# Block 2 of a two-block transformer layer: VectorE takes the next head's maximum ahead of the last head's scaling

## What is computed

```
# branch A, gated_deltanet, per chunk of 64 tokens and head
lmat = where(strict, (k*beta) @ k.T * decay, 0)
tmat = triangular_solve(lmat + eye, eye)     # inverse of a unit triangular matrix
u, w = tmat @ (v*beta), tmat @ (k*beta*exp(gc))

# branch B, dsa_sparse_attention, per block of 128 queries
score  = sum_h iw[h] * relu(iq[h] @ ik.T)    # causal
sel    = top_k(score, 128)                   # keys that are kept
logits = q_b[h] @ ckv[sel].T * R_KV**-0.5 + rel_bias[bucket(dist)]
p      = softmax(logits)                     # over the kept keys, causal
o[h]   = (p @ ckv[sel]) @ w_uv[h];  out = o * silu(z)
```

## Time and profile before

| quantity | value |
|---|---|
| executions | 1872.19, 1874.47, 1874.87 us |
| profiled execution, its own time | 1875.18 us |
| its span in the trace | 1873.4 us, 1.8 us less than its time |
| PE (TensorE matmul) busy | 1765.4 us, 94% of the span |
| DVE (VectorE) busy | 1531.8 us, 82% |
| ACT (ScalarE) busy | 1132.0 us, 60% |
| POOL (GpSimd) busy | 221.8 us, 12% |
| heads and joins side by side | 1703.4 to 1792 us of the span |

### The profile page before, as it was taken

One profiled execution on the slowest core, in us unless ns is written; L12 is line 12 of the kernel. 1 busy time (PEld: TensorE's weight loads), 2 busy tenths in 40 slices (PEclk: granted clock), 3 DMA queues, 4 the chain that ended last, 5 costly groups with the idle time before them and its releaser, 6 DMA issues. The chain is left out here.

```text
span 1873.4 us, 24447 instructions
## 1 busy us (share of the span) xinstructions
PE 1765.4 (94%) x8315; PEld 1382.4 (74%) x8316; DVE 1531.8 (82%) x1732; ACT 1132.0 (60%) x1202; POOL 221.8 (12%) x183
## 2 busy tenths in 40 slices
PE   6988979999999999999999999999999899995888
PEld 3555467888888888888888888888875568874686
DVE  5466668999999999999999999999998477896552
ACT  5353327777777777777777777777764555343431
POOL 0140210000100100100100000010064000102300
PEclk9998969999999999999999999999999899997999
DMA  6023739999999999999999999999987412201001
GB/s 208 28 91 121 305 129 361 408 382 386 381 379 386 388 371 382 393 370 382 396 374 375 395 376 380 387 387 370 388 332 257 141 46 89 90 1 68 1 23 45
DMA packets 104453, 504.57 MB, mean 269 GB/s; under 512 B 18881, under 2 KB 36526, under 8 KB 54130
## 3 DMA queue, kind: packets, MB, share of 16 engines
q1 hardware_dynamic: 97346, 478.22, 66.6%
q0 software_dynamic: 7056, 25.69, 3.9%
HBM read 481.32 MB, written 22.55 MB: 269 GB/s over the span
## 5 line engine op out<-in xcount | busy, mean ns | idle before, releaser
L1771 DVE TENSOR_TENSOR part<-ring,part 128x2048 fp32r<-128x2048 f32 x258 | 585.4, 2292 | 36.1 <-ACT part L1471 36.1
L1471 ACT ACTIVATE part<-ring 128x2048 fp32r<-128x2048 f32 x256 | 486.1, 1920 | 133.9 <-PE bank L1624 75.4
L1601 PE MATMUL bank<-part,xT_hi 128*128 128x512 f32 x1536 | 393.0, 398 | 0.0
L1601 PEld LDWEIGHTS bank<-part,xT_hi 128*128 128x128 f32 x1536 | 284.2, 188 | 59.1
L1471 ACT ACTIVATE part<-rest 128x2048 fp32r<-128x2048 f32 x124 | 238.3, 1923 | 107.8 <-PE bank L1601 81.8
L1771 DVE TENSOR_TENSOR part<-rest,part 128x2048 fp32r<-128x2048 f32 x124 | 281.8, 2300 | 1.3 <-ACT part L1471 1.3
L1635 PE MATMUL bank<-part,actT_hi 128*128 128x512 f32 x1024 | 277.9, 393 | 0.7 <-DVE part L1771 0.5
L1635 PEld LDWEIGHTS bank<-part,actT_hi 128*128 128x128 f32 x1024 | 190.5, 189 | 39.2 <-issue 0.9
L1601 PE MATMUL bank<-part,xT_lo 128*128 128x512 f32 x768 | 205.6, 389 | 0.0
L1928 POOL DMA_INDIRECT rest<-h_rows,rest x33 | 82.6, 2503 | 1031.2 <-PE bank L1584 1015.9
L1601 PEld LDWEIGHTS bank<-part,xT_lo 128*128 128x128 f32 x768 | 144.2, 188 | 30.7
(11 more groups left out here) (516 smaller groups left out, 2465.8 us busy)
## 6 DMA issues: line engine op xcount, KB each, us to landing
ring<-in_w_gate_up SPq DMA_DIRECT2D x194, 1024.0 KB, 7.7
ring<-in_w_down SPq DMA_DIRECT2D x66, 1024.0 KB, 6.8
rest<-in_w_gate_up SPq DMA_DIRECT2D x62, 1024.0 KB, 8.2
rest<-in_w_down SPq DMA_DIRECT2D x62, 1024.0 KB, 7.2
expert_rows<-rest SPq DMA_DIRECT2D x31, 512.0 KB, 8.3
ring<-in_w_in SPq DMA_DIRECT2D x14, 1024.0 KB, 5.2
rest<-in_w_ada SPq DMA_DIRECT2D x8, 1536.0 KB, 7.6
ring<-in_w_out SPq DMA_DIRECT2D x16, 512.0 KB, 6.6
```

The costliest lines, as they stand in the source:

```text
L1471: nc.scalar.activation(hi[part(i, c)], raw(i, c), ACT.Copy).then_inc(sig("hi_ready"), counts)
L1601: ins = nc.tensor.matmul(bank[g][:], rows[:, c, :], w[:, g * 512:(g + 1) * 512], start=first, stop=last, skip_group_check=True)
L1771: V.tensor_tensor(lo[part(i, c)], raw(i, c), hi[part(i, c)].bitcast(F32), ALU.subtract).then_inc(sig("lo_ready"), counts)
```

## The change

VectorE's order alone is rewritten. A new `b_of(j)` takes `logits_of(j)` first, then `probs_of(j - 1)`, the scaling of the head before, then the gate. TensorE, ScalarE and GpSimd keep their streams. In the loop over the joins `step(i - 1)` comes behind the whole of `b_of`.

```diff
+            def b_of(j):
+
+                if j < N_B:
+                    logits_of(j)
+                if 1 <= j <= N_B:
+                    probs_of(j - 1)
+                if 3 <= j < N_B + 3 and (j - 3) % HB == HB - 1:
+                    gate_b((j - 3) // HB)
+
             for j in range(HB):
-                logits_of(j)
+                b_of(j)
                 for k in range(4 * j, min(4 * j + 4, BLOCK - 1)):
                     solve(k)
-                probs_of(j)
             for j in range(HB, AHEAD):
                 expand(2 * (j - HB))
-                logits_of(j)
                 expand(2 * (j - HB) + 1)
-                probs_of(j)
+                b_of(j)
             for i in range(JOINS):
-                j = AHEAD + i
-                if j < N_B:
-                    logits_of(j)
+                b_of(AHEAD + i)
                 if i:
                     step(i - 1)
-                if j < N_B:
-                    probs_of(j)
-                if 3 <= j < N_B + 3 and (j - 3) % HB == HB - 1:
-                    gate_b((j - 3) // HB)
                 if i == 3:
                     w_out_lo_of(1)
```

## The result

The changed kernel takes 1899.15 us (median of 4 runs, 1896.61 to 1905.06) against 1874.18 us before (median of 4): a ratio of 1.014, 95% interval 1.0121 to 1.0158, 25.0 us slower. The forecast was 1894, range 1884 to 1905. The profiled execution is the slowest of the four, 1905.06 us with a span of 1903.2, so a second trace was taken later (`changed_again`, 1898.39 us, span 1896.6).

A forecast was written before the change was run, and what follows sets the result against it. The loop was taken as one chain from `turn` through ScalarE's exponential and VectorE's scaling to TensorE's transposes. 1875.2 us profiled + 14.1 added path + 5 clock falls = 1894.3, so 1894, range 1884 to 1905.

The forecast's parts named there:

- What bounds the loop: Joins' loop: one chain from `turn` through ScalarE's copy and exponential, VectorE's scaling and TensorE's transposes; 16.0 us of transpose waits.
- The added path: Whole stretch: transposes wait for cross product, next head's logits, maximum, reciprocal and scaling; +14.1 us over all turns.
- Ahead of the loop: Before turn 0: head 4's transposes come behind head 5's maximum, so ScalarE's copy slips; +1.3 us, bounds 0 and 2.4.
- Turn 0: First loop turn, 256 keys: from logits issued to transposes 2.70 us against 0.86 before.
- Turns 4 and 5 together: Turn 4 +0.2 us, with `w_out_lo_of(1)` ahead of the maximum; turn 5 -0.3, as its gate comes earlier.
- Turns 6 to 9: Late turns: `turn` to transposes 4.23, 4.29, 4.00 us against 2.10, 2.27, 2.26, +5.9; turn 9 +0.1.
- The clock: TensorE idles in ten turns and falls to 1.2 GHz; three falls of 1.7 us taken, 5 us, bounds 0 and 17.
- one of three gaps: Basis for three falls: of three comparable TensorE idle gaps (2.31, 2.19, 1.50 us), one was followed by a clock fall.
- The clock stays up: Rival for TensorE in the loop: no clock falls, only the path's 14.1 us is paid, 1889; chance 0.20.
- Falls in every turn: Rival for TensorE in the loop: idle time throttles each pass, ten falls of 1.7 us, 1906; chance 0.12.
- Faster: ScalarE stays the last to arrive: Rival: next head's logits and maximum are done before the exponential ends, removed waits win 7.7 us, 1867; chance 0.05.
- No change: Rival: the transposes aren't on the path, so the new order is absorbed, 1875; chance 0.05.

The follow-up runs named there:

- experiment 4: ScalarE's exponential moved ahead of its copy of the turned block: in the changed kernel 1893.38 us, in the kernel before 1864.61 us (ratio 0.9946).
- filled_turns_1_9: Changed kernel plus four TensorE products of 256 columns between logits and transposes in turns 1 to 9, turn 0 unfilled: 1887.01 us, ratio 1.0072 to the kernel before.
- late_0_4: Against the kernel before, only heads 0 to 4 scale behind the next maximum; the joins' loop keeps the old order: 1874.31 us, ratio 1.000.
- logits_first: Changed kernel with TensorE issuing the next head's logits ahead of the join's cross product in the joins' loop: 1886.67 us, ratio 1.0069 to the kernel before.

## Why the prediction came out as it did

- **What bounds the loop** was read rightly: before, ScalarE's exponential is last to arrive at the scaling. Moving it alone (experiment 4) won 10.5 us. The 16.0 us of waits that I took for the size of it were not: 11.6 of them lie ahead of the loop, and the printed waits in it are too short, as experiment 4 shows.
- **The added path.** Predicted 14.1 us, and with the falls of the clock kept away (`filled_turns_1_9`) it is 13.0. That they agree so well is partly luck. Turn by turn the path adds up to 16.1 us:
  - Ahead of the loop I had +1.3; the `turn` that opens turn 0 comes 1.8 later in every trace of the new order.
  - Turn 0, from that `turn` to the transposes, is 4.03 us in the changed kernel and 1.79 in `late_0_4`, which has the old order there, both at 2.4 GHz: 2.2 for 1.8 predicted.
  - Turns 1 to 3 are 5.0 for 5.0.
  - Turns 4 and 5 together cost 0.7 where I had -0.1; the last section says why.
  - Turns 6 to 9 are 6.35 for 6.0. Turn 6 took 4.26 from `turn` to the transposes for 4.23, and `logits_first` 3.43 for 4.29 less 0.89.

  Against these 16.1 stand 3.1 us that half-rate time costs the kernel before and not `filled_turns_1_9`: 1.7 in turn 0, where the clock rose 3 us after head 4's transposes instead of 9, and 1.4 in "end". The prediction had neither. The early rise doesn't follow from the new order alone, since three of the nine traces that have this order up to head 4 have the late one.
- **The clock** is the step that was mis-sized. I took three falls at 1.7, 5 us. The changed kernel's stretch is 7.0 us longer than the filled one's (`filled_turns_1_9`) in the second trace (108.8 less 101.8) and 14.5 in the first (116.3 less 101.8); by the medians, 1899.15 less 1887.01, it is 12. The second trace has just three falls, the first seven. Two of the three cost 1.6 and 1.2 us (7>8 and 8>9), near what I took. What I left out is that a fall need not last 3.3 us: beside turn 9 come small products and a half-rate stretch of 20 us, some 15 of it ahead of the next phase. It alone costs 4.2 us against the filled kernel (14>15 5.8 against 4.8, "end" 11.0 against 7.8). And "one of three gaps" was a thin base that left a row out: the kernel before has a fourth gap, 2.08 us ahead of its next phase, and behind it the clock fell too:

```profile
1793.00:1796.30 3.30, 3.30 (x18) 3.30 (x17) 0.69 (x1) 0.60 (x1) 0.00 (x0) 0.50 0.71 287
```

- **The sum** was 1894.3, measured 1899.15. The clock is 7 us over its term. The other way go the path, 13.0 for 14.1, and the start, a profiled execution 1.0 us above the median of the kernel before.
- **The rivals.** "The clock stays up" (1889) is what `filled_turns_1_9` shows, 1887. "Falls in every turn" (1906) is nearly the first trace, 1905.06, with its seven falls. The Trainium skill's account of a loop that is throttled in each pass ("TensorE: Matmul & The Clock Gate", "HAM oscillation — how this bites in real kernels") fits that trace for five turns running and not the second, where turns 0, 1 and 4 to 8 idle as long and keep the clock. "Faster: ScalarE stays the last to arrive" fell: it was last in one turn of eleven, by 2.0 us. "No change" fell by 25 us.

## What to carry to other kernels

When a stage is reordered so that one engine does the next item's work ahead of the last item's, ask what that work itself waits for: here the maximum of the next head was not free filler, since it needed logits that TensorE issues in the same turn. Find the instruction that arrives last at the wait and move that one; here it was ScalarE's exponential, queued behind a copy that it doesn't need, and moving it alone won 10.5 us where the reordering lost 25. On TensorE, price a new idle time twice, once as path and once for the clock it may cost. The second price is uncertain: here the same kernel lost its clock three times in one execution and seven in another.

## What the runs showed of the hardware

- **A half-rate stretch can outlast busy time.** At the end of the loop TensorE was busy 13.33 of 15.00 us and stayed at 1.2 GHz, and so into the next phase (second trace of the changed kernel, 18.25 busy of 20.10). In that stretch are the 64x64 products; that their size is the reason wasn't tried.
- **Filling idle time pays.** Four products of 256 columns in each of nine turns, some 1.8 us of work a turn that nobody reads, made the kernel 12 us faster (1899.15 to 1887.01).
- **The same instructions met different clocks.** In nine traces TensorE issues the same instructions from the first logits to the `turn` that opens turn 0, at the same distances to 0.1 us (22.1 us to head 4's transposes, 4.2 on to that `turn`). The clock rose 3 us after head 4's transposes in six of them and 9 in three.
- **VectorE and GpSimd held each other up in a chain.** In turn 4, second trace of the changed kernel, VectorE:

```profile
1758.05 2.29 DVE L3369 TENSOR_TENSOR w_out_lo<-ring,w_out_hi 128x2048 fp32r<-128x2048 f32 x1
...
1761.69 1.21 DVE L3357 TENSOR_SCALAR rest<-rest 128x384 f32<-128x384 f32 x1
```

GpSimd beside it:

```profile
1759.27 2.20 POOL L2444 TENSOR_TENSOR ring<-ring,rest 128x512 f32<-128x512 f32 x1 [5.22 <-PE bank L2949]
1761.43 1.25 POOL L2456 TENSOR_TENSOR rest<-rest 128x512 f32<-128x512 f32 x1
```

GpSimd's masking takes 2.20 instead of 1.27 and ends 1.1 us after the subtraction; that makes `sum_bias` late, and its 1.25 us then stretch the scaling from 0.42 to 1.21, on the path. The scaling takes 1.21 to 1.22 us in turn 4 in all three traces looked at (both of the changed kernel, and `filled_turns_1_9`). This is the 0.8 us that turns 4 and 5 had over their sum. The Trainium skill, "SBUF — State Buffer", "Who interferes with whom", states both halves (an instruction with two inputs in SBUF against GpSimd's reads, and one in a two-port mode, where whoever issues first holds the other up). The rows agree: the masking ends 1.13 us after the subtraction, the scaling 0.22 after `sum_bias`. In turns 6 and 7 of the changed kernel the scaling beside `sum_bias` took 0.54 and 0.61 instead of 0.42 and 0.49, the 0.1 that I had given it; turn 4, where the subtraction makes `sum_bias` late, I had missed.
